# Second mixer on one core: projections and state inputs of the sixteen passes as plain float32 products instead of three split products

## What is computed

```python
h = rms_norm_2(x, mix_norm_g)
(u, c_b, c_c, c_x, q, k_c, v_c, k_s, v_s, k_w, v_w, nsa_gates, mix_gates) = split_projection(h @ w_in)
bu = einsum('bsgh,gph->bsgp', u, b_bar)          # state inputs of the state-space branch
states = associative_scan(a, bu); y = einsum('bsgp,ghp->bsgh', states, c).real + d_skip * u
y_ssm = gelu(y) @ w_glu ...                       # y_lin * sigmoid(y_gate)
y_conv = (c_b * causal_conv(c_c * c_x)) @ conv_w_out
y_attn = (compressed, selected and window attention of q over the keys, gated) @ w_o
x = x + (gates_0 * y_ssm + gates_1 * y_conv + gates_2 * y_attn) @ w_out
```

## Time and profile before

| what | before |
|---|---|
| median of 3 runs | 1448.07 us (1447.74 to 1448.14) |
| profiled execution, span | 1447.8 us; 0.3 us under the median |
| PE busy | 1425.5 us, 98% |
| DVE busy | 1153.4 us, 80% |
| ACT busy | 779.5 us, 54% |
| POOL busy | 143.1 us, 10% |
| DMA | 58% of 16 engines, 185 GB/s |

### The profile page before, as it was taken

The page is one execution under the profiler, slowest core; times in us unless marked ns, Lnnn a source line. Parts: engine busy times, 40 slices in busy tenths (PEclk is TensorE's granted clock), DMA queues, the critical chain, the costliest instruction groups (busy, mean ns, idle before and its releaser), DMA issues.

```text
span 1447.8 us, 24184 instructions
## 1 busy us (share of the span) xinstructions
PE 1425.5 (98%) x8485; PEld 1246.2 (86%) x8485; DVE 1153.4 (80%) x1832; ACT 779.5 (54%) x1242; POOL 143.1 (10%) x142
## 2 busy tenths in 40 slices
PE   8999999999999999999999999999999999999999
PEld 7888889888888888888988888888887899888887
DVE  5877777878777787777787988886999976587776
ACT  6444466664444644446667666566544465464442
POOL 0000005100000000001510000022133300000000
PEclk9999999999999999999999999999999999999999
DMA  8666655446665666665545666655634366566562
GB/s 323 217 190 188 194 158 178 156 154 210 197 191 189 213 216 189 193 193 156 180 152 181 206 228 220 218 169 181 219 117 138 110 179 187 174 190 191 187 200 75
DMA packets 73090, 268.05 MB, mean 185 GB/s; under 512 B 8240, under 2 KB 8240, under 8 KB 72752
## 3 DMA queue, kind: packets, MB, share of 16 engines
q1 hardware_dynamic: 69984, 253.79, 55.4%
q10 hardware_dynamic: 3024, 13.15, 2.5%
HBM read 262.71 MB, written 4.19 MB: 184 GB/s over the span
## 4 chain that ended last, share of the span: by engine, by line
PE 90%; DVE 6%; ACT 2%; issue 1%; POOL 1%; DMA 0%; DVEq 0%; ACTq 0%
PE work L777 25%; PE work L778 13%; PE acc L490 9%; PE acc L491 9%; PE acc L492 9%; PE work L490 8%; PE work L491 7%; PE work L492 7%; DVE wlo L476 2%; PE acc L1549 1%; ACT whi L469 1%; PE work L1521 1%; PE work L682 0%; PE acc L675 0%; PE work L1043 0%
## 5 line engine op out<-in xcount | busy, mean ns | idle before, releaser
L469 ACT ACTIVATE whi<-raw 128x1024 fp32r<-128x1024 f32 x480 | 496.9, 1049 | 417.6 <-PE work L778 233.4
L476 DVE TENSOR_TENSOR wlo<-raw,whi 128x1024 fp32r<-128x1024 f32 (+1 forms) x460 | 555.3, 1233 | 43.2 <-ACT whi L469 41.8
L777 PE MATMUL work<-xboth,whi 128*128 128x512 f32 x1600 | 552.3, 391 | 0.0
L778 PE MATMUL work<-xboth,wlo 128*128 128x256 f32 x1600 | 442.2, 276 | 0.0
L777 PEld LDWEIGHTS work<-xboth,whi 128*128 128x128 f32 x1600 | 300.4, 188 | 64.1
L778 PEld LDWEIGHTS work<-xboth,wlo 128*128 128x128 f32 x1600 | 300.4, 188 | 3.7
L490 PE MATMUL acc<-whi,hhi 128*128 128x512 f32 x440 | 173.2, 394 | 0.0
L491 PE MATMUL acc<-wlo,hhi 128*128 128x512 f32 x440 | 172.2, 391 | 0.0
L492 PE MATMUL acc<-whi,hlo 128*128 128x512 f32 x440 | 171.7, 390 | 0.0
L898 DVE TENSOR_REDUCE sg<-work 128x256 f32<-128x512 f32 x100 | 69.1, 691 | 78.6 <-PE work L778 78.5
L490 PE MATMUL work<-xboth,whi 128*128 128x256 f32 (+1 forms) x424 | 121.1, 286 | 0.0
(11 more groups left out here) (457 smaller groups left out, 2100.8 us busy)
## 6 DMA issues: line engine op xcount, KB each, us to landing
raw<-stream SPq DMA_DIRECT2D x480, 512.0 KB, 4.1
par<-pm ACTq DMA_DIRECT2D x2, 1644.5 KB, 7.6
spilled<-rotated ACTq DMA_DIRECT2D x6, 512.0 KB, 5.7
pfa<-pf_a ACTq DMA_DIRECT2D x3, 516.0 KB, 4.3
table<-spilled ACTq DMA_DIRECT2D x3, 512.0 KB, 3.2
par<-spilled ACTq DMA_DIRECT2D x3, 512.0 KB, 3.3
pfb<-pf_b ACTq DMA_DIRECT2D x2, 516.0 KB, 8.6
x<-x_in SPq DMA_DIRECT2D x2, 512.0 KB, 6.0
```

Of the source, the lines that this page charges most:

```text
L469: nc.scalar.activation(chunk(whi, place, c)[:, cols], chunk(raw, place, c)[:, cols], ACT.Copy).then_inc(hi_ready, 1)
L476: nc.vector.tensor_tensor(chunk(wlo, place, c)[:, cols], chunk(raw, place, c)[:, cols], chunk(whi, place, c)[:, cols].bitcast(F32), ALU.su ...
L777: nc.tensor.matmul(o[:, :], hi[:, k * P:(k + 1) * P], xboth[:, k, :], start=k == 0, stop=False)
L778: m = nc.tensor.matmul(o[:, 0:S], lo[:, k * P:(k + 1) * P], xhi[:, k, :], start=False, stop=k == KD - 1)
```

## The change

Twenty chunks of the second mixer are declared `NATIVE`: the channel chunks of the 16 passes and the four `D_B` chunks. They are not split. PE multiplies the raw float32 chunk with a float32 activation in one product where there were three: the channels with `x32`, which POOL makes by adding the high and the low part of the normed input, the state inputs with `uT` itself. The split of `uT` into `y5hi` and `y5lo` ahead of the passes goes. The count of split chunks no longer equals the chunk's number (`Place.split`). SP's loop is cut in three, and in the second mixer it issues its transfers one by one; a load into the slot of an unsplit chunk waits for `consumed` in place of `lo_ready`. On POOL the four sums come first, and the key norm's power moves behind the coefficients. Some small tiles now share memory with tiles that are no longer used (`pcT`, `pc`, `ce`, `y5t`).

```diff
+NATIVE = sorted(CHANNEL_CHUNK[AHEAD:AHEAD + 16] + D_B)
...
+    def split(self, c):
+
+        return self.rounds * RING + (self.base + c + 1 - self.before - sum(n <= c for n in self.native))
...
         def split_hi(act, place, cs):
             for c in cs:
+                if c in place.native:
+                    continue
...
         def split_lo(dve, place, cs):
             for c in cs:
+                if c in place.native:
+                    continue
...
             def channels(name, c, n=P):
                 begin2(pe, name)
-                pe.wait_ge(lo_ready, place.count(c))
+                if c in place.native:
+                    pe.wait_ge(arrived[place.slot(c)], place.loaded(c))
+                    x32_ready.wait(pe, 4)
+                    whole = chunk(raw, place, c)
+                    for k in range(KD):
+                        m = nc.tensor.matmul(bank2(name, slice(0, S)), whole[:, k * P:(k + 1) * P], x32[:, k, :], start=k == 0, stop=k == KD - 1)
+                    m.then_inc(consumed, 1)
+                    return
+                pe.wait_ge(lo_ready, place.split(c))
...
-            uhl_ready.wait(pe, 4)
+            evac2.wait(pe, BY_ACT2.index("u3") + 1)
             wc_ready.wait(pe, 1)
...
-                pe.wait_ge(lo_ready, place.count(c))
+                pe.wait_ge(arrived[place.slot(c)], place.loaded(c))
                 for i in range(2):
                     at = slice((r % 4 * 2 + i) * P, (r % 4 * 2 + i + 1) * P)
-                    m = product(bank2(f"bu{r}", slice(i * S, (i + 1) * S)), chunk(whi, place, c)[:, at], chunk(wlo, place, c)[:, at],
-                                y5hi[:, r // 4, :], y5lo[:, r // 4, :], True, True)
+                    m = nc.tensor.matmul(bank2(f"bu{r}", slice(i * S, (i + 1) * S)), chunk(raw, place, c)[:, at], uT[:, r // 4, :], start=True, stop=True)
...
-            evac2.wait(act, evac2.k)
-            for b in range(4):
-                ucopy.inc(nc.scalar.activation(y5hi[:, b, :], uT[:, b, :], ACT.Copy))
...
+            pool.wait_ge(xlo_ready, 6 * 8 + 8)
+            for i in range(4):
+                both = xboth[:, 2 * i:2 * i + 2, :].bitcast(F32)
+                x32_ready.inc(nc.gpsimd.tensor_tensor(x32[:, 2 * i:2 * i + 2, :], both[:, :, 0:S], both[:, :, S:2 * S], ALU.add))
             s5m.wait(pool, 1)
             mean_pow(rstds[:, :, 0:8], means[:, :, 0:8], 8)
-            s5m.wait(pool, 2)
-            mean_pow(rstds[:, :, 8:12], means[:, :, 8:12], 4)
             pool.wait_ge(turns_stored, 96)
...
             wc_ready.inc(nc.gpsimd.tensor_copy(cre, a3))
+            s5m.wait(pool, 2)
+            mean_pow(rstds[:, :, 8:12], means[:, :, 8:12], 4)
             s5m.wait(pool, 3)
...
-            for b in range(4):
-                ucopy.wait(dve, b + 1)
-                uhl_ready.inc(tt(y5lo[:, b, :], uT[:, b, :], y5hi[:, b, :].bitcast(F32), ALU.subtract))
...
+            for c in range(FFN3_BASE + RING - MIX2_BASE):
+                if c - RING in NATIVE:
+                    sp.wait_ge(consumed, mix2_place.count(c - RING) + RING)
+                else:
+                    sp.wait_ge(lo_ready, mix2_place.split(c - RING))
+                sp.dma_start(chunk(raw, mix2_place, c), stream[MIX2_BASE + c]).then_inc(arrived[mix2_place.slot(c)], 16)
```

More of the change, by code:

```diff
@@ L472, in split_lo @@
             for c in cs:
+                if c in place.native:
+                    continue
                 cols = used(place, c)
-                dve.wait_ge(hi_ready, place.count(c))
+                dve.wait_ge(hi_ready, place.split(c))
                 nc.vector.tensor_tensor(chunk(wlo, place, c)[:, cols], chunk(raw, place, c)[:, cols], chunk(whi, place, c)[:, cols].bitcast(F32),
@@ L479, in split_lo_pool @@
         def split_lo_pool(pool, place, cs):
-            pool.wait_ge(lo_ready, place.count(cs[0] - 1))
+            pool.wait_ge(lo_ready, place.split(cs[0] - 1))
             for c in cs:
                 cols = used(place, c)
-                pool.wait_ge(hi_ready, place.count(c))
+                pool.wait_ge(hi_ready, place.split(c))
                 nc.gpsimd.tensor_tensor(chunk(wlo, place, c)[:, cols], chunk(raw, place, c)[:, cols], chunk(whi, place, c)[:, cols].bitcast(F32),
@@ L713, in held @@
                     if (t, h) == (0, 0):
-                        pe.wait_ge(lo_ready, at.count(c))
+                        pe.wait_ge(lo_ready, at.split(c))
                         ready(n)
@@ L754, in head @@
                     if t == 0:
-                        pe.wait_ge(lo_ready, place.count(c + step - 1))
+                        pe.wait_ge(lo_ready, place.split(c + step - 1))
                     for k in range(KD):
@@ L989, in tokens @@
                     if k == 0 or ((k + 1) * n - 1) // CH > (k * n - 1) // CH:
-                        pe.wait_ge(lo_ready, place.count(c + ((k + 1) * n - 1) // CH))
+                        pe.wait_ge(lo_ready, place.split(c + ((k + 1) * n - 1) // CH))
                     if first:
@@ L1102, in mix_pe @@
                     turned_out("ybt", yb, AB)
-                pe.wait_ge(lo_ready, place.count(C_OUT + i))
+                pe.wait_ge(lo_ready, place.split(C_OUT + i))
                 y_lo.wait(pe, need[i])
@@ L1305, in mix_dve @@
             weights(0)
-            dve.wait_ge(lo_ready, place.count(C_UV - 1))
+            dve.wait_ge(lo_ready, place.split(C_UV - 1))
             split_lo(dve, place, [C_UV, C_UV + 1])
```

36 lines of the change are left out of this document (21 added, 15 removed).

## The result

| | before | after |
|---|---|---|
| median, first comparison (5 runs each) | 1448.07 us (1447.74 to 1448.57) | 1453.73 us (1453.07 to 1454.32) |
| ratio | | 1.0038 [1.0026, 1.0051] |
| median, repeated on another chip | 1448.11 us (17 runs) | 1453.35 us (6 runs) |
| ratio | | 1.0032 [1.0020, 1.0044] |
| span of the profiled execution | 1447.8 us | 1452.0 us |

The change makes the kernel slower by 5.2 to 5.7 us between medians. The profiled spans differ by 4.2 us only. Every execution whose span is listed takes about 1.7 us more than its span, and the listed ones of the kernel before fall into two groups: spans of 1446.0 to 1446.6 us at a mean granted clock of 1.000, and 1447.0 to 1448.1 us at 0.999. The profile of before (1447.8 us) belongs to the second group. The median of the first comparison, less 1.7 us, is 1446.4 us and fits the first.

A forecast was written before the change was run, and what follows sets the result against it. PE, busy in 98% of the span, was taken as the bound. 9.3 + 2.4 - 5.9 - 1.3 + 0.6 = +5.1 us on 1448.07 us gave 1453.2 us, with an 8-in-10 range of 1449.5 to 1459.5 us.

The forecast's parts named there:

- The channels, +9.3 us: In each of 16 passes, 24 split products become eight plain ones, costing PE 0.58 us a pass, +9.3 us.
- The state inputs, +2.4 us: In each of 16 passes, six products become two of 0.43 us, costing PE 0.15 us a pass, +2.4 us.
- Waits in and after the passes, -5.9 us: In and right after the passes, DVE loses 22 us of work and all 5.9 us of PE waits go.
- The wait near 1022 us, -1.3 us: Ahead of the passes, DVE reaches the split at 1022.81 us earlier, so PE's wait goes with its drain, -1.3 us.
- The coefficients and sums at their new place, 0: At about 963 to 992 us, POOL's moved coefficients and new sums may slow DVE at most 14 us; booked as nothing.
- The transfers, +0.6 us: Late chunk loads in passes 11 to 15 hold ACT, chiefly in pass 15: +0.6 us, ends 0 and +1.5.
- I expect both to stay: The 1.47 us wait at 1048.24 us and the lower clock behind it, costing 1.7 us, both remain.
- signs of being wrong: Plain products closer than 0.40 us, a pair of passes under 13 us, or PE waiting for ACT in passes 12 to 15.
- second rival: Plain products cost 0.23 us each, as with 32-column weights, so the kernel gets faster, about 1422 us; chance 0.05.
- the first (no change): The 1048.24 us wait and lower clock go too, plain groups cost less, transfers nothing: 1448.5 us; chance 0.12.
- The third (late chunks delay the softmax in passes 11 to 15): Each wait of ACT for a landing delays a softmax, five times 1 to 1.5 us: 1459 to 1460 us; chance 0.15.

The follow-up runs named there:

- inputs_only: Changed kernel with only the four state-input chunks unsplit, channels split as before and no sums on GpSimd: 1443.95 us.
- split_kept: Changed kernel, but ScalarE and VectorE split the twenty chunks as before though nobody reads the split parts: 1453.41 us.
- reorder_only: Kernel before with only the key norm's power moved behind the output coefficients on GpSimd: 1446.61 us.
- no_reorder: Changed kernel with the key norm's power moved back ahead of the output coefficients on GpSimd: 1453.65 us.
- tail_order: Changed kernel, but ScalarE splits the last chunk named for pass 15 after copying that pass's transposed weights: 1452.68 us.
- late_compressed: Version with only state inputs unsplit, plus compressed-attention transposes moved behind pass 0's first channel and their products into pass 1: 1443.94 us.
- weights_first: Version with only state inputs unsplit, plus both compressed score products ahead of channel 7 and chunk 37's split behind the small DVE operations: 1443.98 us.
- channels_only: Changed kernel with only the channels unsplit; state inputs keep their split and three products: 1451.82 us.

## Why the prediction was right

The forecast was 1453.2 us; 1453.73 us was measured, and 1453.35 us when repeated. The mechanism held: PE's added work was larger than the waits that it could remove. That the sum fits within 0.6 us is in part luck, since terms that were booked too low on either side cancel. The terms:

- **The channels, +9.3 us.** Right in kind, a little low. A pair of passes takes 14.15 us against 12.58, which is 0.785 us a pass. The channel gives 0.54, the state inputs 0.15, and 0.08 to 0.09 lie in the transposes between them: the step at the head of the split group, booked in the 0.53 to 0.63, is still paid, one step earlier. It comes with the plain channel, not with the state inputs: in inputs_only the four transposes take 0.36 us (1084.64 to 1085.00). A plain channel therefore costs 0.62 us a pass. Times 16, both terms are 12.6 us, against 11.7 forecast.
- **The state inputs, +2.4 us.** 0.86 against 0.71 us, as forecast.
- **Waits in and after the passes, -5.9 us.** The waits went, 4.2 us of them in the six pairs, and DVE is busy for 76.0 us, near the 80 forecast. But the reason given, DVE relieved by 22 us, was not needed: split_kept gives DVE most of that work back and PE still does not wait. The longer passes and the dropped wait of PE for the splits hide it. One wait was not booked: the 0.48 us at 1050 us that reorder_only shows and the changed kernel does not.
- **The wait near 1022 us, -1.3 us.** Right: 1.5 us by position, and 1.5 us measured by reorder_only alone. The order on GpSimd is enough for it (reorder_only), and so is the rest of the change (no_reorder).
- **The coefficients and sums at their new place, 0.** Right for PE. DVE's busy time rose by 9 us there, within the 14 us named as the most, and PE's did not change.
- **The transfers, +0.6 us.** The mechanism was right and the place exact, after pass 15; the wait is 0.81 us, and tail_order gets 0.7 us back.
- **"I expect both to stay"** for the wait at 1048.24 and the lower clock behind it is the step that failed. The wait stayed, 1.31 us. The clock did not fall: 1.00 over 1045 to 1055 us, where the earlier trace rows had 0.83, and none of the 11 listed executions of the changed kernel shows 0.999. It did not fall in reorder_only either, with the wait still at 1.47 us, so the lower clock went with the coefficients' new place and not with the length of this wait. It was also worth less than the 1.7 us booked: from the wait's end to the compressed products PE took 4.60 us in the profile of before (1048.24 to 1052.84) and 3.72 us in reorder_only (1046.31 to 1050.03), in which the wait of 0.48 us is contained. And it is no gain in the median: the median of before in the first comparison fits the full clock. I had taken the profiled execution for a run 0.3 us under the median, when its span was 1.4 us above the one that belongs to the median. The error of the baseline hid the error of the step.

Put on the median's footing, the sum is 12.6 (products), -0.15 (pass 0, hidden in its wait), -5.9, -0.5 (the wait at 1050 us), -1.5, and +0.9 for the new wait: about +5.5, against 5.2 to 5.7 measured. The profile of reorder_only, at full clock and with its first product of the mixer at 953.00 like the changed kernel's, confirms it by position. The changed kernel takes 0.7 us more up to the first state output, 5.3 more over the six pairs and 1.0 more up to the last: 7.0 us between the spans (1445.0 and 1452.0). That is the same sum without the -1.5 us that both have.

None of the signs of being wrong came: plain products stand 0.43 us apart and a pair takes 14.15 us. From pass 12 on PE waits for ACT only once, for the values of pass 15, which come behind the last pass; that wait was booked. One step of arithmetic in the second rival is rounded: 160 products times 0.03 us are 4.8 us, and the 5.1 us need 0.032.

Of the rivals, the first (no change) needed the wait at 1048 us to go too, and it stayed; of its parts only the lower clock went, which was not in the median. The second (plain products at 0.23 us) is out: they stand 0.43 us apart. The third (late chunks delay the softmax in passes 11 to 15) found its late chunks, with ACT waiting up to 3.4 us for them, but PE met only the last. Its own time was also a little off: five times 1 to 1.5 us on top of 1453.2 us is 1458 to 1461 us.

## What to carry to other kernels

When the engine on the chain is nearly full, price an exchange of its work against its own waits first: here 12.6 us of added products stood against about 7.5 us of waits, and relieving a neighbour could not change the sign. Take the cheapest unit of relief and stop when the waits are gone: unsplitting the four state-input chunks costs PE 2.4 us and ends nearly all of those in the passes (with the new order on GpSimd 1443.95 us, under both kernels and 2.7 us under the new order alone), while the sixteen channels cost 0.62 us each and buy almost nothing. Before trusting a profile as the baseline, compare its granted clock and span with those of the timed runs.

## What the runs showed of the hardware that was not expected

Four DVE subtractions of 128x256 took 5.09 us beside GpSimd's coefficient operations and 1.42 us alone, a factor of 3.6, far more than the 6.30 against 3.49 us of the large splits. And the kernel before ran with two spans about 1.4 us apart: in 13 of 20 executions of one group, 4 of 17 and 5 of 16 of the others, the mean granted clock was 0.999, in the rest 1.000. In its profile the clock falls to the lower level after PE's wait of 1.47 us at 1048 us; in the changed kernel, with a wait of 1.31 us at the same place, none of the listed executions showed it. The length of this one wait does not decide it: reorder_only has the same 1.47 us and never fell in 11 executions, late_compressed has 1.67 us and never fell in 6, and weights_first, with 1.62 us, shows 0.999 in three of six. In channels_only the profile keeps the full clock behind a wait of 1.46 us at 1046.55 and falls behind one of 1.45 us at 1159.53. What sets the kernel before apart is its other wait, 1.15 us at 1022.81, 25 us earlier, which is gone in reorder_only and in the changed kernel; that this is the reason is not shown.
